# Long convolution: second signal turned early into its own buffers, later filter spectra summed on GpSimd, PSUM sets taken in another order, raw queries and keys copied out of PSUM

## What is computed

```python
z = short_conv(u @ w_in + b_in, conv_w, conv_b)     # width 3, 3072 channels
x0, x1, v = jnp.split(z, 3, axis=-1)
s = (v * x1).astype(jnp.float32)
g = hyena_filter(L, ...)       # 3 small layers with sines, then taps with a decay
y = jnp.fft.irfft(jnp.fft.rfft(s, n=n, axis=1) * jnp.fft.rfft(g, n=n, axis=0)[None],
                  n=n, axis=1)[:, :L]
y = (y + s * skip.astype(jnp.float32)).astype(u.dtype) * x0
return y @ w_out + b_out
```

```python
q = rms_norm(q, g_qn)          # per token and head
k = rms_norm(k, g_kn)
```

## Time and profile before

| | |
|---|---|
| median of 3 executions | 2016.24 us (2015.15 to 2017.19) |
| profiled execution, own time | 2016.88 us |
| its span, first to last instruction | 2015.1 us |
| PE busy | 1925.5 us, 96% of the span |
| DVE, ACT, POOL busy | 48%, 35%, 45% |
| mean granted clock of PE | 0.981 of full speed |

### The profile page before, as it was taken

The page is one execution under the profiler, slowest core; times in us unless marked ns, Lnnn a source line. Parts: engine busy times, 40 slices in busy tenths (PEclk is TensorE's granted clock), DMA queues, the critical chain, the costliest instruction groups (busy, mean ns, idle before and its releaser), DMA issues.

```text
span 2015.1 us, 23041 instructions
## 1 busy us (share of the span) xinstructions
PE 1925.5 (96%) x8775; PEld 1579.0 (78%) x8775; DVE 969.8 (48%) x1271; ACT 699.3 (35%) x1028; POOL 911.9 (45%) x410
## 2 busy tenths in 40 slices
PE   7899779999999998899989999999999899999999
PEld 5677668888888887678868888888788778888887
DVE  6765683544431136555565454311865564544301
ACT  4444333323223344454453233222225443332211
POOL 3464333444444443463534444444535435544442
PEclk9999899999999999899999999999999999999999
DMA  4232012332322322202313323223233223233222
GB/s 157 76 101 82 0 63 84 105 96 91 104 84 89 113 81 84 75 9 84 105 63 105 99 88 104 86 92 112 92 107 109 99 63 103 84 104 96 84 97 78
DMA packets 165064, 178.91 MB, mean 89 GB/s; under 512 B 4584, under 2 KB 152544, under 8 KB 164737
## 3 DMA queue, kind: packets, MB, share of 16 engines
q1 hardware_dynamic: 161996, 172.08, 26.5%
q10 hardware_dynamic: 2997, 5.84, 0.9%
HBM read 175.82 MB, written 2.10 MB: 88 GB/s over the span
## 4 chain that ended last, share of the span: by engine, by line
PE 27%; issue 20%; POOL 9%; DVE 3%; ACT 1%; POOLq 0%; DVEq 0%
POOL w_lo L2191 9%; PE acc L522 8%; PE acc L524 8%; PE acc L523 8%; PE aux L597 1%; PE acc L870 0%; PE aux L522 0%; PE aux L523 0%; PE aux L524 0%; DVE a_lo L1118 0%; PE aux L923 0%; DVE x L1139 0%; PE acc L877 0%; ACT a_hi L1773 0%; DVE small L1098 0%
## 5 line engine op out<-in xcount | busy, mean ns | idle before, releaser
L2191 POOL TENSOR_TENSOR w_lo<-w_raw,w_hi 128x1024 fp32r<-128x1024 f32 x326 | 802.6, 2483 | 988.4 <-ACT w_hi L1751 988.4
L522 PE MATMUL acc<-a_hi,w_hi 128*128 128x512 f32 (+1 forms) x1480 | 583.0, 394 | 2.9 <-DVE a_lo L1118 1.4
L523 PE MATMUL acc<-a_lo,w_hi 128*128 128x512 f32 (+1 forms) x1480 | 577.9, 390 | 0.0
L524 PE MATMUL acc<-a_hi,w_lo 128*128 128x512 f32 (+1 forms) x1480 | 577.6, 390 | 0.0
L1751 ACT ACTIVATE w_hi<-w_raw 128x1024 fp32r<-128x1024 f32 x326 | 327.0, 1051 | 490.3 <-PE acc L524 464.4
L522 PEld LDWEIGHTS acc<-a_hi,w_hi 128*128 128x128 f32 (+1 forms) x1480 | 278.1, 188 | 72.2 <-issue 9.2
L524 PEld LDWEIGHTS acc<-a_hi,w_lo 128*128 128x128 f32 (+1 forms) x1480 | 278.1, 188 | 59.6
L523 PEld LDWEIGHTS acc<-a_lo,w_hi 128*128 128x128 f32 (+1 forms) x1480 | 278.2, 188 | 58.8 <-issue 1.4
L522 PE MATMUL acc<-h_hi,w_hi 128*128 128x512 f32 x528 | 205.8, 390 | 0.0
L524 PE MATMUL acc<-h_hi,w_lo 128*128 128x512 f32 x528 | 205.4, 389 | 0.0
L523 PE MATMUL acc<-h_lo,w_hi 128*128 128x512 f32 x528 | 205.4, 389 | 0.0
(11 more groups left out here) (401 smaller groups left out, 2419.2 us busy)
## 6 DMA issues: line engine op xcount, KB each, us to landing
w_raw<-in_w_gate SPq DMA_DIRECT2D x22, 1024.0 KB, 5.1
w_raw<-in_w_up SPq DMA_DIRECT2D x22, 1024.0 KB, 5.2
w_raw<-in_w_down SPq DMA_DIRECT2D x16, 896.0 KB, 5.0
w_raw<-in_hy_w_in SPq DMA_DIRECT2D x12, 1024.0 KB, 4.9
w_raw<-in_ffn_w_gate SPq DMA_DIRECT2D x11, 1024.0 KB, 5.1
w_raw<-in_ffn_w_up SPq DMA_DIRECT2D x11, 1024.0 KB, 5.1
w_raw<-in_e_w_in SPq DMA_DIRECT2D x10, 1024.0 KB, 5.0
w_raw<-in_xa_wkv SPq DMA_DIRECT2D x8, 1024.0 KB, 5.1
```

The source lines that it names most:

```text
L522: nc.tensor.matmul(o, l_hi, r_hi, start=start, stop=False)
L523: nc.tensor.matmul(o, l_hi, r_lo, start=False, stop=False)
L524: return nc.tensor.matmul(o, l_lo, r_hi, start=False, stop=stop)
L2191: nc.gpsimd.tensor_tensor(w_lo[s][:, half], w_raw[s][:, half], w_hi[s][:, half].bitcast(F32), ALU.subtract)\
```

## The change

The filter network's argument stays in its PSUM bank while DVE works on it. ACT converts the next weight block behind both middle-weight steps of a block instead of between them, and POOL forms its remainder behind the tap sums. The second signal has buffers `s_hi`, `s_lo` of its own, in the region of `eo`, and is turned between S of the first half's two frequency groups. ACT therefore waits there until POOL has read all of `eo`. The filter spectra of the second half are copied out of PSUM by ACT (`filter_copy`) and summed by POOL (`filter_sums` there). The rest of the sequence alternates acc and aux. Raw queries and keys are copied out of PSUM by ACT, which frees the banks, and DVE scales them in SBUF.

```diff
+    s_hi = [s_hi, at("s_hi1", [P, TT, HALF], F32R, offset=x_at)]
+    s_lo = [s_lo, at("s_lo1", [P, TT, HALF], F32R, offset=x_at + 4 * TT * HALF)]
...
         forward("S", 0, 0, True)
+        pe.wait_ge(acc_free, 24)
+        signal(1)
         forward("S", 0, 1, False)
         pe.wait_ge(eo_ready, 4 * TT)
         forward("G", 1, 0, True)
-        signal(1)
-        forward("G", 1, 1, True)
         aux_result(("s", 1, TT - 1))
-        forward("S", 1, 0, False)
-        forward("S", 1, 1, True)
-        block_done(20)
+        forward("S", 1, 0, True)
+        forward("G", 1, 1, False)
+        forward("S", 1, 1, False)
+        block_done(16 + 1)
         pe.wait_ge(in_x_again, 16)
         for k in range(KT):
-            transposes(("x again", k), [x_again[:, t, k * P:(k + 1) * P] for t in range(TT)])
+            transposes(("x again", k), [x_again[:, t, k * P:(k + 1) * P] for t in range(TT)], in_acc=True)
         inv_hi, inv_lo = block_in(4, T, whole=True)
-        inverse(0, False)
-        inverse(1, True)
+        inverse(0, True)
+        inverse(1, False)
...
         def head_transposes(name, raw):
-            acc_result((name, TT - 1))
+            pe.wait_ge(raw_scaled, 1 if name == "q" else 2)
...
         def layer_argument(j):
-            bank = take_aux()
-            free_aux(V.tensor_scalar(hbuf[:, :], bank[0:64, :], par("hy_f_b%d" % (j + 1), rows=64),
-                                     par("hy_f_freq", rows=64), ALU.add, ALU.mult), again=True)
+            h = take_aux()[0:64, :]
+            step(V.tensor_scalar(h, h, par("hy_f_b%d" % (j + 1), rows=64), par("hy_f_freq", rows=64), ALU.add, ALU.mult))
             magic = 1.5 * 2.0 ** 23
-            step(V.tensor_scalar(kbuf[:, :], hbuf[:, :], 1.0 / (2 * math.pi), magic, ALU.mult, ALU.add))
+            step(V.tensor_scalar(kbuf[:, :], h, 1.0 / (2 * math.pi), magic, ALU.mult, ALU.add))
             step(V.tensor_scalar(kbuf[:, :], kbuf[:, :], -magic, None, ALU.add))
             for part in TWO_PI:
-                step(V.scalar_tensor_tensor(hbuf[:, :], kbuf[:, :], -part, hbuf[:, :], ALU.mult, ALU.add))
-            for_act(V.tensor_scalar(hbuf[:, :], hbuf[:, :], PI_BELOW, -PI_BELOW, ALU.min, ALU.max))
+                step(V.scalar_tensor_tensor(h, kbuf[:, :], -part, h, ALU.mult, ALU.add))
+            ins = V.tensor_scalar(hbuf[:, :], h, PI_BELOW, -PI_BELOW, ALU.min, ALU.max)
+            free_aux(ins)
...
-        products(0, 0, True)
+        products(0, 0, True, inside=lambda: signal(1))
         signal_sums(False)
         products(0, 1, False)
-        filter_sums(0, True)
-        signal(1)
-        filter_sums(1, True)
-        signal_sums(False)
-        products(1, 0, False)
-        signal_sums(True, last=step)
-        products(1, 1, True)
+        sums_elsewhere(True)
+        signal_sums(True)
+        products(1, 0, True)
+        sums_elsewhere(False)
+        signal_sums(False, last=step)
+        products(1, 1, False)
...
-                free_acc(V.tensor_tensor(by_head(raw[:, t, :]), by_head(bank), scale, ALU.mult))
+                ins = V.tensor_tensor(by_head(raw[:, t, :]), by_head(raw[:, t, :]), scale, ALU.mult)
...
             for e in range(2):
                 if e:
-                    split_next()
                     if b in (1, 2):
                         sine(b)
...
+            split_next()
             if b in TAPS_AFTER:
                 windows(*TAPS_AFTER[b])
...
             banks = banks_of(("s", half, TT - 1))
-            result(S.activation(s_hi[:, :, :], banks[:, :, :], ACT.Copy))
+            if half:
+                act.wait_ge(eo_ready, 4 * TT)
+            result(S.activation(s_hi[half][:, :, :], banks[:, :, :], ACT.Copy))
...
+        def filter_copy(f, in_acc):
+            given()
+            banks = banks_of(("G", 1, f, 3))
+            S.activation(g_pm[:, f, 0, :, :], banks[:, 0:2, :], ACT.Copy)
+            S.activation(odd_part[:, :, :], banks[:, 2:4, :], ACT.Copy).then_inc(acc_free if in_acc else aux_free, 4)
...
                 result(S.activation(tmp[t][:, :], acc[:, n % 4, :], ACT.Square))
+                act.wait_ge(acc_free, n)
+                S.activation(raw[:, t, :], acc[:, n % 4, :], ACT.Copy).then_inc(acc_free, 1)
...
         for b in range(12):
-            lo_half(b % 2)
             if b - 1 in TAPS_AFTER:
                 half, n = TAPS_AFTER[b - 1]
                 add_taps(half, n)
                 if half == 0:
                     even_odd_lo(n)
+            lo_half(b % 2)
...
+        def filter_sums(f, freed, marks):
+            pool.wait_ge(freed, marks[("G", 1, f, 3)] + 1)
+            nc.gpsimd.tensor_tensor(g_pm[:, f, 1, :, :], g_pm[:, f, 0, :, :], odd_part[:, :, :], ALU.subtract)
+            nc.gpsimd.tensor_tensor(g_pm[:, f, 0, :, :], g_pm[:, f, 0, :, :], odd_part[:, :, :], ALU.add)\
+                .then_inc(g_summed, 1)
```

More of the change, by code:

```diff
@@ L591, in stats_columns, with transposes @@
             last.then_inc(aux_ready, 1)
-        def transposes(name, parts):
-            bank = open_aux(name)
+        def transposes(name, parts, in_acc=False):
+            bank = open_acc(name) if in_acc else open_aux(name)
             for j, part in enumerate(parts):
@@ L695, in forward @@
                     else:
-                        r_hi, r_lo = s_hi, s_lo
+                        r_hi, r_lo = s_hi[half], s_lo[half]
                     bank = open_acc(name) if in_acc else open_aux(name)
@@ L1256, in signal @@
             acted()
-            free_four(V.tensor_tensor(s_lo[:, :, :], banks[:, :, :], s_hi[:, :, :].bitcast(F32), ALU.subtract), False)
+            free_four(V.tensor_tensor(s_lo[half][:, :, :], banks[:, :, :], s_hi[half][:, :, :].bitcast(F32), ALU.subtract), False)
         def filter_sums(f, in_acc):
@@ L1276, in signal_sums, with sums_elsewhere, products @@
             settle()
-        def products(half, f, in_acc):
+        def sums_elsewhere(in_acc):
+            done, freed, count = (acc_done, acc_read, n_acc) if in_acc else (aux_done, aux_read, n_aux)
+            done.next(4)
+            freed.next(4)
+            count[0] += 4
+        def products(half, f, in_acc, inside=None):
             banks = acc if in_acc else aux
             raw = y_raw[half]
+            if half:
+                dve.wait_ge(g_summed, f + 1)
             for sign in range(2):
+                if sign and inside:
+                    inside()
                 b = 2 * sign
@@ L1466, in normalized_heads @@
             root(mult[:, cs], row_sums[:, cs], 1, (half[:, cs], square[:, cs]), psum=False, eps=0.0)
-            for t, bank in zip(range(first, end), banks):
+            n_acc[0] += end - first
+            acc_done.next(end - first)
+            dve.wait_ge(acc_free, acc_read.next(end - first))
+            for t in range(first, end):
                 scale = mult[:, 8 * t:8 * t + 8].rearrange("p (h one) -> p h one", one=1).to_broadcast([P, HEADS, HD])
-                free_acc(V.tensor_tensor(by_head(raw[:, t, :]), by_head(bank), scale, ALU.mult))
+                ins = V.tensor_tensor(by_head(raw[:, t, :]), by_head(raw[:, t, :]), scale, ALU.mult)
+            (signal_with if end == TT else lambda ins, _: step(ins))(ins, scaled)
         def heads_low(hi, lo, gain):
@@ L1898, in _ @@
         odd_copy("S", 0, 0)
+        signal(1)
         given()
         odd_copy("S", 0, 1)
+        act.dma_start(x_again[:, :, :], ins["x"][0].rearrange("(t p) d -> p t d", p=P)).then_inc(in_x_again, 16)
         spectrum_high(0, 0)
[L1902 to L1903 removed]
+        filter_copy(0, True)
+        act.wait_ge(g_summed, 1)
+        odd_copy("S", 1, 0)
         spectrum_high(0, 1)
[L1905 to L1918 removed]
+        filter_copy(1, False)
+        act.wait_ge(g_summed, 2)
+        odd_copy("S", 1, 1)
+        for k in range(KT):
+            n = acc_mark[("x again", k)]
+            act.wait_ge(acc_ready, n + 1)
+            S.activation(x[:, k, :], acc[:, n % 4, :], ACT.Copy).then_inc(acc_free, 1)
+        spectrum_high(1, 0)
+        split_next()
         spectrum_high(1, 1)
```

74 lines of the change are left out of this document (33 added, 41 removed).

## The result

The changed kernel takes 1989.39 us (median of 4, 1988.56 to 1991.67), the kernel before 2016.72 (median of 4, 2015.15 to 2017.29): ratio 0.9871, 95% interval 0.9858 to 0.9883. That is 26 us less by the ratio and 27.3 by the medians. The forecast was 1985, so the sum of 31.7 us was 4 to 6 us too large: the time lies in the stated range of 1980 to 1996, but outside the 1981 to 1988 that had a chance of 0.55. The profiled execution took 1989.65 us.

A forecast was written before the change was run, and what follows sets the result against it. PE was taken to bound the kernel, busy 1925.5 of 2015.1 us, with its waits and the low clock behind them as the loss. Terms 4.3 + 15.4 + 12.0 = 31.7 off 2016.88 gave 1985 us, range 1980 to 1996.

The forecast's parts named there:

- These 35 us are what the change can touch: PE's waits early on and at queries and keys: their total, 35 us, is what the change can affect.
- Part 1: Filter network and moved conversions: sine sooner through PSUM, block 2 later; 4.3 us gained, bounds 0 and 6.
- Parts 2 to 4: Long convolution from its start to the first inverse, with the second signal early: 15.4 us gained, bounds 9 and 18.
- The second G ends at 198.6: Start of the long convolution: second G done at 198.6 us, after PE waits of 1.3 and 0.4 around the tap norms.
- Rival (b): Second signal: the new wait eats more, through low clock or POOL's sums; 1991 or 1995 us, chance 0.15.
- DVE sets the pace: Long convolution after the second signal's long wait: DVE bounds it, one `products` 10.2 us, `signal_sums` 2.5.
- The tail: Behind the first inverse, where DVE's remainders of `c` meet POOL's weight halves: unchanged.
- Part 5: Queries and keys: freed banks shrink two stretches to 5.44 us each; 12.0 us gained, bounds 7 and 12.5.
- In the old times it ends the queries' root at 796.05 and the scaling of the last pair at 797.3: Queries: DVE's times from before, giving scaling done at 797.8 us, before PE arrives at 798.2.
- rival (c): Queries and keys: POOL catches the SBUF scaling, 4 us lost at each; 1989 to 1993 us, chance 0.10.
- The rest: The program behind gates, queries, keys and values: 0 us of change.
- (a): In-projection: moved conversions cost as much as the sine gives, first term zero or less; 1989 to 1991 us, chance 0.12.

The follow-up runs named there:

- net_psum: Kernel before with only the filter network's argument kept in its PSUM bank, conversions left between the two middle weights: 2012.34 us, ratio 0.9986.
- arg_sbuf: Changed kernel with the filter network's argument back in SBUF (`hbuf`): 1988.88 us, ratio 0.9862.
- signal_first: Changed kernel, but ACT copies `s_hi` of the first signal before it converts the next weight block: 1986.86 us, ratio 0.9853.
- even_first: Changed kernel; ACT rounds two `eo` tiles earlier, DVE forms the second `s_lo` ahead of `products`, POOL forms the last `e_lo` before the last `o_lo`: 1989.30 us.
- qk_alone: Kernel before with only the queries and keys change (ACT copies them raw from PSUM, DVE scales in SBUF): 2007.17 us, ratio 0.9958.
- low_later: Changed kernel, but DVE forms the first three `ye_lo` behind the queries' second scaling: 1987.50 us, ratio 0.9858.
- two: Changed kernel; ACT copies the first signal's `s_hi` before the last conversion, DVE forms `ye_lo` behind the queries' scaling and last spatial gate: 1987.57 us, ratio 0.9852.
- split_moved: Kernel before with only the conversions moved behind both outputs and POOL's tap work ahead of `lo_half`: 2007.44 us, ratio 0.9963.

## Why the prediction came out as it did

**The first paragraph.** "These 35 us are what the change can touch" is a slip. The earlier trace rows have the wait of 8.7 us twice, not three times, and with the 4.6 and the earlier trace rows the waits named there add up to 39.7. No term of the sum rests on it.

**Part 1, 4.3 against 5.2.** Block 2 started at 48.23 (forecast 48.7) behind a wait of 3.9 (4.4), the sine was ready at 54.4 (55.1) and no later block waited. The size was right; in eight more kernels with this order the stage gained 4.7 to 7.1. The mechanism was only half right: I gave the 4.05 us to PSUM. PSUM alone gives them (`net_psum`), but so does the moved conversion alone (`arg_sbuf`), and together they give them once. I had priced the moved conversion as a pure cost of 3.3 us, and never asked what it does to POOL's time.

**Parts 2 to 4, 15.4 against 12.9.** The waits came as forecast within 0.5 us. The step that failed is "The second G ends at 198.6", by the clock: it ended 7.2 us after its start, not 5.5, from a low level of 3.4 us behind waits that I thought too small (`signal_first`: without the wait of 1.4, 5.6 us). On the forecast's clock that G ended 2.2 us late and the first inverse came 2.5 late, so nearly all of the error is there. Rival (b) asked about the clock behind the long wait; that one was as priced, S of the second group took 7.5 us for 7.7. "DVE sets the pace" was too simple. Behind the long wait PE waited 2.2 and 2.1 us for copies by ACT and only 0.7 for DVE, and DVE was idle for 2.8, 0.6 and 1.6 us ahead of its signal sums. With S earlier, PE waits for banks that DVE holds, then DVE waits for PE, 3.9 us by the trace of `even_first`. The work goes in a ring through PE, ACT and DVE, and no one engine's time sets it.

**The tail, "unchanged", gained 1.3.** The waits are unchanged, the clock behind them is not. This was luck: from the first inverse to the gates it took 494.6 us before and 493.4 in the changed kernel, but 494.8 in `arg_sbuf`, with the same code there.

**Part 5, 12.0 against 8.0** (9.6 with the 1.6 of the gates' clock). The step that failed is "In the old times it ends the queries' root at 796.05 and the scaling of the last pair at 797.3". I moved PE's times forward and left POOL's meeting with DVE where it was. In before, `ye_lo` was through 0.15 us ahead of POOL. In the changed kernel it was caught, and with it the scaling: a wait of 2.45 and the clock behind it (3.60 us at a granted clock of 0.54), which make the 4 us that rival (c) gave for one of its two places, though (c) had meant root steps and not these; the keys had room, as two root steps of 2.3 us were caught there without a wait. `qk_alone` kept the old meeting and gave 12.2. So the size of (c) was right, and the meeting on which it hangs was not worked out. The Trainium skill (SBUF — State Buffer, Who interferes with whom) says that the instruction which starts first holds the shared ports to its end, and the other stands still. The rows agree: a root step of 0.18 us takes 2.3, about one POOL instruction of 2.4.

**The rest, 0 against -1.5.** The same instructions took 1166.3 us in the kernel before, 1167.8 in the changed one and 1170.1 in `qk_alone`, and from 1166.2 (`low_later`) to 1171.0 (`arg_sbuf`, `two`) over all fourteen traces. About half or more of it is busy time of PE, from low-clock stretches that fall on other work; what sets where they fall stays open. I had no term for it, and no row of before could have given one.

Of the rivals only (c) came true, and only at the queries, where it took 4 us. (a) did not: `split_moved` gained 7.5. (b) did not either: the 2 us of the second G were lost ahead of the long wait, which no rival had. That the range held the time is in part luck: gains that I had not forecast, 0.9 in part 1, 1.3 in the tail and 1.6 at the gates, stand against losses of 2.5, 4.0 and 1.5.

## What to carry to other kernels

When an edit moves an engine in time, list which steps of DVE with all operands in SBUF stand within a few tenths of a microsecond of a POOL instruction, and move those that nobody needs soon out of the way; a margin of 0.15 us is no margin. A long wait in a ring of engines may be nearly free, so cut first a short one that nothing behind it takes back (1.4 us gave 3.0 in its stage, 4.8 gave about 1.0). Give work to the slower engine when the faster one holds what PE waits for, and leave up to 5 us in the range for the part that the change does not touch.

## What the runs showed of the hardware

- A stretch of 32 small matmuls ran in 3.8 us (four kernels) or in about 5.4 (seven), with the same code there. In all eleven this went with whether DVE's two steps 11 us later took 5.7 us or 1.4.
- `low_later` and the changed kernel have the same code up to the gates. Yet the tap norms started at 184.19 in one and at 186.05 in the other, by where the low clock fell: in `low_later` at 20 to 30 us (granted clock 0.83), ahead of block 2, which then waited 1.6 us and ran at 1.00; in the changed kernel behind block 2's wait of 3.9 (0.83 from 50 to 58 us). From the first signal transposes to the first inverse the same code took 75.5 (`arg_sbuf`), 75.8 and 77.0 us. A single trace does not settle a gain of 2 us at a distance, nor one of 1 us within a stage.
- The step on 128 x 2 elements with a single tensor input, 1.85 us in the earlier trace rows, took 1.82 in the changed kernel (46.38, beside POOL's `w_lo` from 45.83) and 0.17 a few us earlier and later. The root step of 2.29 in the earlier trace rows has a single tensor input as well. So steps with one SBUF input are caught too. A reduction from SBUF was not: at 780.12 in the kernel before it took its usual 0.69 us with `w_lo` running from 777.87 to 782.63.
